# Positions brought in for all 128 partitions by one transfer, and the rope angles computed before the first row scales

## The reference, cut to what matters

```
def _rope(x, positions):                      # applied to q_a, k_a, q_i, k_i, q_r, k_r
    freqs = ROPE_THETA ** (-arange(half) / half)
    ang = positions[..., None] * freqs        # positions: (1, 512) int32
    return concat([x1*cos(ang) - x2*sin(ang), x2*cos(ang) + x1*sin(ang)])

mod = silu(c) @ w_ada + b_ada                 # shift1, scale1, gate1, shift2, scale2, gate2
h = _rms_norm(x, g_pre_mix) * (1 + scale1) + shift1
x = x + gate1 * _rms_norm(_hybrid_mixer(h, positions, w_in, w_out), g_post_mix)
h2 = _rms_norm(x, g_pre_ffn) * (1 + scale2) + shift2
out = x + gate2 * _rms_norm(_hier_moe(h2, ...), g_post_ffn)
```

## Time and profile before

| | |
|---|---|
| Median of 3 runs | 664.86 us (664.17 to 666.93) |
| The profiled execution: its own time / its span | 665.48 us / 663.7 us |
| Busy in the span: PE, DVE, ACT, POOL | 624.7 (94%), 376.2 (57%), 206.2 (31%), 101.8 (15%) us |
| Transfers | 174.44 MB, mean 263 GB/s |
| Mean granted TensorE clock | 0.988 of 2.4 GHz |

### The profile page before, as it was taken

The page is one execution under the profiler, slowest core; times in us unless marked ns, Lnnn a source line. Parts: engine busy times, 40 slices in busy tenths (PEclk is TensorE's granted clock), DMA queues, the critical chain, the costliest instruction groups (busy, mean ns, idle before and its releaser), DMA issues.

```text
span 663.7 us, 7108 instructions
## 1 busy us (share of the span) xinstructions
PE 624.7 (94%) x2407; PEld 296.6 (45%) x2407; DVE 376.2 (57%) x717; ACT 206.2 (31%) x410; POOL 101.8 (15%) x96
## 2 busy tenths in 40 slices
PE   5999999999999999999999999989999999989791
PEld 3664444443444444456644474434343454433230
DVE  4858968999986763246861469743224242332056
ACT  5406434434354535421121250112122131222023
POOL 1006433300233320000000001021211212110001
PEclk9899999999999999999999998999999999999997
DMA  9996551513307062161397659599999999999997
GB/s 321 382 381 218 200 190 64 195 58 108 148 1 253 1 232 88 49 214 33 124 385 326 241 197 390 185 407 406 421 421 419 420 420 420 418 420 411 409 402 139
DMA packets 52135, 174.44 MB, mean 263 GB/s; under 512 B 9577, under 2 KB 9729, under 8 KB 41730
## 3 DMA queue, kind: packets, MB, share of 16 engines
q1 hardware_dynamic: 45024, 160.26, 62.1%
q0 software_dynamic: 6160, 12.10, 5.7%
q10 hardware_dynamic: 914, 1.61, 0.7%
HBM read 168.17 MB, written 15.21 MB: 276 GB/s over the span
## 4 chain that ended last, share of the span: by engine, by line
PE 75%; DVE 13%; DMA 4%; ACT 2%; issue 2%; SPq 1%; ACTq 0%; DVEq 0%
PE psum L814 17%; PE psum L1148 16%; PE psum L1209 9%; PE psum L815 8%; PE psum L1007 8%; DVE score L1654 2%; DMA ring<-in_w_down_exp 2%; PE psum L1118 2%; DVE sm L1653 2%; DVE score L1884 2%; DVE rows L1554 2%; PE psum L984 2%; PE psum L964 2%; PE psum L972 2%; SPq L585 1%
## 5 line engine op out<-in xcount | busy, mean ns | idle before, releaser
L814 PE MATMUL psum<-hT,ring 128*128 128x512 f32 (+1 forms) x320 | 135.6, 576 | 0.0
L814 PEld LDWEIGHTS psum<-hT,ring 128*128 128x128 f32 x320 | 59.4, 190 | 68.4 <-issue 60.1
L1148 PE MATMUL psum<-ring,hT 128*64 128x512 f32 (+2 forms) x320 | 85.3, 595 | 4.2 <-DMA ring<-in_w_up_exp 3.8
L815 PE MATMUL psum<-ring,hT 128*128 128x512 f32 x192 | 85.2, 597 | 0.0
L2005 DVE TENSOR_SCALAR work<-work 128x256 f32<-128x256 f32 x16 | 4.6, 290 | 96.9 <-PE psum L1158 71.1
L1554 DVE SCALAR_TENSOR_TENSOR rows<-ring,sm,rows 128x512 f32<-128x512 f32 x64 | 56.1, 876 | 1.7
L1351 ACT ACTIVATE both_bufs<-psum 32x512 f32<-32x512 f32 (+2 forms) x68 | 38.3, 563 | 60.1 <-PE psum L814 56.5
L815 PEld LDWEIGHTS psum<-ring,hT 128*128 128x128 f32 x192 | 35.6, 190 | 44.6 <-issue 44.2
L1450 ACT ACTIVATE work<-psum 128x256 f32<-128x256 f32 x17 | 6.5, 383 | 142.9 <-PE psum L1148 142.9
L1148 PEld LDWEIGHTS psum<-ring,hT 128*64 128x64 f32 (+2 forms) x320 | 28.0, 137 | 48.2 <-issue 46.0
L1209 PE MATMUL psum<-ring,work 128*64 128x512 f32 (+1 forms) x160 | 40.1, 598 | 1.2 <-ACT work L1456 1.2
(11 more groups left out here) (325 smaller groups left out, 906.9 us busy)
## 6 DMA issues: line engine op xcount, KB each, us to landing
ring<-in_w_down_exp SPq DMA_DIRECT2D x20, 1024.0 KB, 21.6
ring<-in_w_ada SPq DMA_DIRECT2D x8, 2048.0 KB, 13.2
ring<-in_w_in SPq DMA_DIRECT2D x7, 2048.0 KB, 8.8
ring<-in_w_gate_exp SPq DMA_DIRECT2D x12, 1024.0 KB, 20.5
ring<-in_w_up_exp SPq DMA_DIRECT2D x12, 1024.0 KB, 25.1
ring<-in_w_ada SPq DMA_DIRECT2D x16, 512.0 KB, 10.2
ring<-in_w_gate_exp SPq DMA_DIRECT2D x16, 512.0 KB, 13.9
ring<-in_w_up_exp SPq DMA_DIRECT2D x16, 512.0 KB, 13.8
```

The costliest lines, as they stand in the source:

```text
L814: return pe.matmul(o[:, at], w[:, k, b * P:(b + 1) * P], hT3[:, k, at], **ends)
L815: return pe.matmul(o[:, :], hT3[:, k, b * P:(b + 1) * P], w[:, k, :], **ends)
L1148: mm = pe.matmul(o[rows, :], XT[u % 2][:, k, rows], both(GU_SLOT[place])[:, k, :, :], start=(k == 0), stop=(k == KD - 1))
```

## The change

The positions come in one transfer that reads the 512 numbers once for each of the 128 partitions, issued by SP as its second, ahead of x. DVE converts them for all partitions at once and makes the angles directly behind, before the bias rows are copied. The one-partition copy, the product on PE that spread them, its copy out of PSUM and ACT's transfer go. The ten `warm` products behind the transposes become eight.

```
@@ Plan
-        use(("positions",), 1)
@@ read_out
-                    "positions": lambda: (ang_ready, 1),
@@ block.sync
             sp.dma_start(cst[:, 0:SOON_CONST], t["cst"][:, 0:SOON_CONST]).then_inc(cst_in, 16)
+            sp.dma_start(posi, prow(t["positions"], S)).then_inc(pos_in, 16)
             for b in range(NB):
                 sp.dma_start(x3[:, b, :], x_blocks[b]).then_inc(rows_in[b], 16)
@@ block.tensor
-            def spread_positions():
-
-                o = take(pe, ("positions",))
-                pe.wait_ge(pos_row, 1)
-                pe.matmul(o[:, :], ones[0:1, :], turns[0:1, :], start=True, stop=True).then_inc(modA_done, 1)
...
             turn_raw_rows()
-            spread_positions()
...
-            warm(10)
+            warm(8)
             sum_first(0)
@@ block.scalar
-            act.dma_start(posi[0:1, :], t["positions"]).then_inc(pos_in, 16)
@@ block.vector, first_norm
-                dve.wait_ge(modA_done, min(pair + 3, 5))
+                dve.wait_ge(modA_done, min(pair + 2, 4))
@@ block.vector
             dve.wait_ge(pos_in, 16)
-            v.tensor_copy(turns[0:1, :], posi[0:1, :]).then_inc(pos_row, 1)
+            link(v.tensor_copy(posf, posi))
+            dve.wait_ge(cst_in, 16)
+            reduce_angles(0)
+            finish_angles(0)
             dve.wait_ge(modA_done, 1)
             link(v.tensor_copy(cgb, bank(("modA",))[:, 16:40]))
-            dve.wait_ge(cst_in, 16)
-            dve.wait_ge(modA_done, 2)
-            link(v.tensor_copy(posf, bank(("positions",))))
-            reduce_angles(0)
-            finish_angles(0)
```

More of the change, by code:

```diff
@@ L403, in build @@
         first_in = [sem(f"first_in{i}") for i in range(2 * PIECES - 1)]
-        x_evA, x_evV, pos_row = sem("x_evA"), sem("x_evV"), sem("pos_row")
+        x_evA, x_evV = sem("x_evA"), sem("x_evV")
         x_ss, x_r, x_n = sem("x_ss"), sem("x_r"), sem("x_n")
```

## The result

The changed kernel takes 667.54 us (median of 22 runs, 664.89 to 670.41) against 664.9 us (22 runs, 663.02 to 666.93). The ratio is 1.0038, 95% interval 1.0025 to 1.005: slower by 2.5 us, within the half per cent I had named, but outside my range of 662.3 to 666.6 and on the other side of the forecast. The mean granted clock of its runs is 0.985. Time and clock go together in them: eight executions have a mean clock of 0.983 or less and take 667.97 to 670.41 us, four have 0.989 and take 664.89 to 665.74, within 1 us of the median before. Of the 70 runs of the kernel before that stand beside the experiments none has a clock under 0.984. The profiled execution took 666.54 us; its span is 664.7, only 1.0 longer than before.

The account below looks back on a forecast made before the run. Bound: a first-stage chain from DVE's angles through ACT and PE to the first sum, afterwards w_ada and DVE. -1.6 + 0.85 = -0.75 us took the profiled 665.48 to 664.7, median 664.1; range 662.3 to 666.6.

Parts of the forecast that it names:

- Angles, cast, hand-over: On DVE, cast 0.45 and angles 5.23 us, ending at 10.4; ACT then normalizes from 13.1 instead of 15.66.
- PE ready, DVE the bound: PE is ready for the first sum about 22, but DVE's w_ada products end at 24.8; sum at 24.85.
- The base and the new transfer: -1.6: First modulation sum starts at 24.85 instead of 26.46, with the new transfer's delay counted: 1.6 us earlier.
- The 0.66 for the new transfer: The positions' 262 KB, ahead of x, make everything behind them in the transfers 0.66 us later.
- The clock, +0.85: PE's idle time ahead of the sum brings 3.4 us at half clock, costing 1.7; half charged, 0.85.
- rival 1: Low clock around the sum, granted twice, up to 6.8 us: 666.7; decides from 3.2 us PE-bound; chance 0.17.
- the place at 408: At 408.4, PE idled 0.94 us, then did 16 two-column records; clock 0.50 for 3.4 us; taken as comparison.
- Passing on to the end: An advance at the first projection (28.68) was taken to reach the kernel's end whole.
- Rivals 2 to 4: Alternatives: full gain (0.20), slow positions transfer (0.07), gain taken back later by DVE or a transfer (0.06).
- The whole gain: Clock stays up or falls only while PE idles: -1.6 to -2.3, 662.6 to 663.3; chance 0.20.
- The slow transfer: Positions, one row read 128 times, delay 2.65 instead of 0.66: net +0.35, 665.2; chance 0.07.
- Rival 4: Change works but DVE or a transfer later takes the gain back before the end: 664.9; chance 0.06.

Follow-up runs that it names:

- experiment 9: The kernel before, unchanged, one execution for a second trace; 665.8 us.
- experiments 2 and 3: The kernel before with fewer products without a result than its 10: 8 in the former (665.58 us, ratio 1.001), 2 in the latter (668.0 us, ratio 1.0045).
- experiment 1: The changed kernel with 14 products without a result behind the transposes instead of 8; 665.3 us, ratio 1.001.
- experiment 5: The changed kernel once more, unchanged; 667.81 us, ratio 1.005 against the kernel before.
- experiment 8: The changed kernel with four more products without a result behind the wait for DVE, ahead of the sum; 667.44 us, ratio 1.0051.
- experiment 7: The changed kernel with 14 products without a result and the positions' transfer issued by ACT instead of SP; 664.78 us, ratio 1.0005.

## Why the prediction was wrong, point by point

- *Angles, cast, hand-over.* Right. Cast 0.43 (predicted 0.45); the instructions of the angles, which are nine and not ten, 6.39 to 11.63, that is 5.24 (5.23). They ended at 11.6, not 10.4: the positions came at 5.9, not 4.5, within the bounds. ACT's first normalized block at 12.96 (13.1). What I did not see in the path removed: that PE's product of positions began at 7.40 and no earlier because `b_ada` landed late in that execution (experiment 9).
- *PE ready, DVE the bound.* PE at 22.02 (22), last product ends 24.69 (24.8), the sum starts 24.73 (24.85). The idle gap was there as forecast.
- *The base and the new transfer: -1.6.* This step failed. I took "the sum starts at 26.46" for the kernel; in a second trace and in experiments 2 and 3 it starts at 24.6, behind DVE. So the advance, the main term, mostly did not exist: it is 24.6 before against 24.7 to 25.2 after. That also answers experiment 1, which restores before and doesn't beat it. The 0.66 for the new transfer rests on the same trace. Against the earlier trace rows the eighth piece is 0.5 later; against the other traces with the old transfers (20.1 to 20.4) it is 1.6 to 2.4 later with the wide transfer on SP's queue (21.97, 22.4, 22.5). How much of this the transfer causes is not shown, as two traces of before differ by 1.4 without it; why their transfers land at different times I did not test.
- *The clock, +0.85.* This step failed as well, by size. I let one low stretch of 3.4 us fall half into waiting. Measured: 6.8 us in both traces, in the first all but 0.2 of it where PE is the bound, worth some 3 us (18.15 from first to second sum against 14.93 in the earlier trace rows and 15.19 in experiment 1's trace, which waits for DVE too). I had described this as rival 1, with the right place, the right length and the point of decision (3.2 us of PE-bound time), and gave it 0.17, because low stretches had been 3.4 us until then. The rival's time, 666.7, is short too, since it has the same -1.6 in it. And its reason, a sum at half clock in which PE shows too little work, isn't shown: in experiment 5 the sum ran at full clock for the most part, the low level came behind it, under a PE without gaps, and lasted as long.
- *What separates the traces* is how long PE is idle ahead of the first sum. In the four with 2.71 us or more (the changed kernel twice, experiments 3 and 8) the low level lasts 6.8 us or longer; in the ten with 1.10 us or less it lasts 3.4 us somewhere in front, or isn't there. No trace lies between, and why the long idle time brings two such lengths stays open. My comparison was with the place at 408, where PE had been idle 0.94 us: "only longer", I wrote, and did not charge for it.
- *Sum by what was measured.* The second sum holds both terms. It stands at 42.88 and 43.53 in the changed kernel, at 41.39 and 41.51 in the kernel before: 1.4 to 2.1 later, beside a measured 2.5 (1.7 to 3.3).
- *Passing on to the end.* From the second sum to the late two-column products is 365.4 us before, after and in experiment 1. So up to there a delay passes on, and an advance too: experiment 1 has these products at 405.80, experiment 7 at 405.08, and before has 406.74. Behind them it can't be followed in single traces. The gather of rows that comes next takes 6.2 to 7.8 us in the 14 traces, kernels of both kinds (6.21 before, 7.60 in experiment 7, which leaves 0.4 of 1.7 us), and from the start of PE's last products to the end it is 14.3 to 16.4. That is as large as what was looked for. Low stretches near 163 and between 615 and 626 come and go in the same way. That the advance reaches the end whole is thus not shown: experiment 7's front is 2 us ahead in two traces, and its ratio excludes 2 us.
- *Rivals 2 to 4.* The whole gain is excluded by the result. The slow transfer: 4.75 us to land against 5.3, but hidden, as DVE's reciprocal waited for ACT's square root until 12.75. Rival 4, a gain taken back later, had no gain to act on in the changed kernel; for experiment 7 it is not excluded. The Trainium skill (page "Trainium Kernel Development and Optimization", Key Constraints) has it that a second issuing queue only saves issue time. The traces don't contradict it: on ACT's queue w_ada landed 0.3 to 1.0 us earlier than with SP's transfer, whose issue took 0.42; the rest no run here takes apart.

## What to carry to other kernels

Before taking filler out of TensorE's queue, ask what it will wait for next: where the bound moves to another engine or a transfer, the time freed turns into an idle gap, and the gap can cost more than it held. Put the filler in the gap, sized to end just as the awaited work does; four products behind the gap gained nothing here. And take the base of a sum of single microseconds from more than one trace: here two executions of one kernel had nearly the same total and fronts that differed by 1.8 us at the place that mattered. Follow a chain to its first transfer, too: the start of the product that I took out was set, in the trace that I read, by a transfer that has nothing to do with the positions.

## What was not expected of the hardware

The low level (1.2 GHz) lasted 3.4 us in some places, 6.8 in others and over 13 in one, with PE reported 94% busy under the last. In experiment 5 it came 1.5 us after PE had begun to work again and stayed for 6.8 us under a PE without gaps; in experiment 8 eight records of 256 columns right behind the idle time, then one-column records, did not bring the clock back. Both are single executions.
